# Interleaved map rows, a split rotary swap and earlier value splits in the projection of a hybrid attention kernel

## The reference, cut to what matters

```python
def partial_rope(t, positions):
    half = ROPE_DIM // 2          # ROPE_DIM = 16, half = 8
    ...
    x1, x2, rest = tf[..., :half], tf[..., half:ROPE_DIM], tf[..., ROPE_DIM:]
    return jnp.concatenate([x1 * cos - x2 * sin, x2 * cos + x1 * sin, rest], axis=-1)

proj = h @ w_in[layer]
dq = proj[..., :o1].reshape(b, s, 2 * DIFF_HEADS, HEAD_DIM)     # HEAD_DIM = 64
dk = proj[..., o1:o2].reshape(b, s, 2 * DIFF_HEADS, HEAD_DIM)
dv = proj[..., o2:o3].reshape(b, s, DIFF_HEADS, DIFF_V_DIM).astype(f32)
dq = partial_rope(dq, positions)
dk = partial_rope(dk, positions)
```

## Time and profile before

| | us |
|---|---|
| median of 3 runs (lowest, highest) | 3023.31 (3022.39, 3024.48) |
| the profiled execution, its time | 3015.76 |
| the profiled execution, its span (first to last instruction) | 3013.7 |
| TensorE matmuls (PE) busy | 2917.5, 97% of the span |
| VectorE (DVE) busy | 1972.6, 65% |
| ScalarE (ACT) busy | 1586.0, 53% |
| GpSimd (POOL) busy | 913.2, 30% |
| granted TensorE clock, mean | 0.994 of full speed |

### The profile page before, as it was taken

How to read it: one execution, slowest core, us unless ns; L and a number is a source line. 1 busy time by engine, 2 the same in 40 slices (tenths; PEclk the granted TensorE clock), 3 DMA queues, 4 the chain that set the end, 5 groups by cost and what they waited for, 6 DMA issues and landing times.

```text
span 3013.7 us, 51920 instructions
## 1 busy us (share of the span) xinstructions
PE 2917.5 (97%) x19000; PEld 2610.4 (87%) x19000; DVE 1972.6 (65%) x2944; ACT 1586.0 (53%) x2672; POOL 913.2 (30%) x1022
## 2 busy tenths in 40 slices
PE   7999989899999999999999999999999999999998
PEld 6888778787777999999889998998889998999886
DVE  6215520177676777778568786886658878888656
ACT  5122211267767878888545554554445555655444
POOL 1922221055665877777301221111000000001100
PEclk9999999999999999999999999999999999999999
DMA  5488895556643541501339998999746775699954
GB/s 206 123 212 206 206 234 131 128 114 149 149 108 66 122 88 25 113 32 61 109 126 286 315 308 255 281 274 311 213 131 217 233 237 182 217 327 295 286 191 157
DMA packets 303481, 559.47 MB, mean 186 GB/s; under 512 B 32288, under 2 KB 70304, under 8 KB 302112
## 3 DMA queue, kind: packets, MB, share of 16 engines
q1 hardware_dynamic: 263936, 464.17, 48.6%
q0 software_dynamic: 39072, 92.30, 16.0%
q10 hardware_dynamic: 288, 0.59, 0.1%
HBM read 449.98 MB, written 197.13 MB: 215 GB/s over the span
## 4 chain that ended last, share of the span: by engine, by line
PE 61%; DVE 9%; POOL 5%; ACT 3%; issue 2%; DMA 1%; DVEq 0%; SPq 0%; ACTq 0%; POOLq 0%
PE f_ps L2428 28%; PE f_ps L2320 18%; PE h_o L996 6%; PE h_t L982 3%; PE h_z L718 2%; PE h_z L721 2%; POOL h_work L1280 2%; DVE h_negmax L1116 2%; POOL h_more L1280 2%; DVE h_more L1232 2%; DVE h_more L1148 1%; ACT h_more L1015 1%; ACT h_work L1015 1%; POOL h_srstd L1325 1%; PE h_o L939 0%
## 5 line engine op out<-in xcount | busy, mean ns | idle before, releaser
L1807 ACT ACTIVATE f_whi<-f_wraw 128x512 fp32r<-128x512 f32 x834 | 520.9, 627 | 420.0 <-PE f_ps L2428 288.9
L1814 DVE TENSOR_TENSOR f_wlo<-f_wraw,f_whi 128x512 fp32r<-128x512 f32 x834 | 574.8, 690 | 240.8 <-ACT f_whi L1807 237.7
L2428 PE MATMUL f_ps<-f_hi_s,f_whi 128*128 128x256 f32 x1408 | 397.3, 282 | 4.7 <-DVE f_up L2161 4.7
L2428 PE MATMUL f_ps<-f_lo_s,f_whi 128*128 128x256 f32 x1408 | 397.2, 282 | 0.0
L2428 PE MATMUL f_ps<-f_hi_s,f_wlo 128*128 128x256 f32 x1408 | 396.5, 282 | 0.0
L1320 POOL TENSOR_TENSOR h_work<-h_work,h_more 128x1024 f32<-128x1024 f32 (+3 forms) x192 | 302.6, 1589 | 110.0 <-DVE h_more L1232 97.2
L2428 PE MATMUL f_ps<-f_hi_a,f_whi 128*128 128x256 f32 x1056 | 298.3, 282 | 1.1 <-DVE f_second L2161 0.8
L2428 PE MATMUL f_ps<-f_lo_a,f_whi 128*128 128x256 f32 x1056 | 297.9, 282 | 0.0
L2428 PE MATMUL f_ps<-f_hi_a,f_wlo 128*128 128x256 f32 x1056 | 297.7, 282 | 0.0
L2428 PEld LDWEIGHTS f_ps<-f_hi_s,f_whi 128*128 128x128 f32 x1408 | 267.6, 190 | 5.6 <-DVE f_wlo L1814 3.1
L2428 PEld LDWEIGHTS f_ps<-f_hi_s,f_wlo 128*128 128x128 f32 x1408 | 267.6, 190 | 0.0
(11 more groups left out here) (199 smaller groups left out, 6874.2 us busy)
## 6 DMA issues: line engine op xcount, KB each, us to landing
f_wraw<-in_w_stream SPq DMA_DIRECT2D x394, 256.0 KB, 4.0
f_wraw<-sums_scratch SPq DMA_DIRECT2D x352, 256.0 KB, 4.4
sums_scratch<-in_w_stream POOLq DMA_DIRECT2D x132, 256.0 KB, 5.4
act_scratch<-f_act SPq DMA_DIRECT2D x88, 256.0 KB, 3.8
combined_acts<-f_act SPq DMA_DIRECT2D x88, 256.0 KB, 4.7
f_wraw<-down_sums SPq DMA_DIRECT2D x88, 256.0 KB, 2.7
f_piece<-combined_acts SPq DMA_DIRECT2D x88, 256.0 KB, 2.9
down_sums<-in_w_stream POOLq DMA_DIRECT2D x66, 256.0 KB, 6.5
```

The lines of the kernel that those rows point to most:

```text
L1807: act.activation(w_hi[ring][:], w_raw[ring][:], ACT.Copy).then_inc(S["hi_split"], 1)
L1814: dve.tensor_tensor(w_lo[ring][:], w_raw[ring][:], w_hi[ring][:].bitcast(F32), ALU.subtract).then_inc(S["lo_split"], 1)
L2428: mm = pe.matmul(outs[i], w[ring][:, col], a[name][:, c, :], start=(c == 0 and m == 0), stop=(c == 3 and m == 2))
```

## The change

- The columns of the query and key weights are reordered ahead of the run, for all 16 tiles: row 2y + m of a tile is now row y of map m. The first halves of both maps (8 rows each) are then rows 0 to 15, the second halves rows 16 to 31. `inv_freq` follows.
- The store writes the rows back in their old order in memory: its memory side is given as (64 rows, 2 maps, 512 tokens). Nothing that reads the scratch changes. All 64 units are stored this way.
- The swap is two transfers of 16 rows: second halves to first by SP, first halves to second by ScalarE's queue, right behind the copy, with a wait for that copy. The counts on `swapped` fall from 64 to 32 per unit.
- VectorE makes raw times cosine first, after the copy and ahead of the wait for the transfers; sine is multiplied into `swapped_qk` in place.
- `V_SPLITS` gives one value split to each of units 57 to 61 and two to unit 62; splits 3 to 5 wait for the sum of a unit and not for its low part; value loads 4 to 7 are issued behind units 57 to 60, one each.
- ScalarE waits once, ahead of unit 32, for the cleared `swapped_qk`.

```diff
--- before.py
+++ after.py
@@ -68,7 +68,8 @@
 UNITS = TILES * BLOCKS
 HALVES = 2 * TPB
 TURNED = HEAD_DIM // 8
-V_SPLITS = {UNITS - 6: (0,), UNITS - 5: (1,), UNITS - 4: (2, 3), UNITS - 3: (4,), UNITS - 2: (5, 6)}
+FIRST_HALVES, SECOND_HALVES = slice(0, 2 * TURNED), slice(2 * TURNED, 4 * TURNED)
+V_SPLITS = {UNITS - 7: (0,), UNITS - 6: (1,), UNITS - 5: (2,), UNITS - 4: (3,), UNITS - 3: (4,), UNITS - 2: (5, 6)}
 
 
 SUM_OPS = 8
@@ -192,18 +193,14 @@
                 n, b = unit_of(o)
                 sp.wait_ge(unit_done, BLOCKS + o + 1)
                 for part_no, src in ((0, out_hi), (1, out_lo)):
-                    sp.dma_start(qk_scratch[part_no, n * P:(n + 1) * P, b * BLK:(b + 1) * BLK],
-                                 src[:, b, :].bitcast(F32)).then_inc(stored[b], 16)
+                    rows = qk_scratch[part_no, n * P:(n + 1) * P, b * BLK:(b + 1) * BLK]
+                    sp.dma_start(rows.rearrange("(m y) t -> y m t", m=2), src[:, b, :].bitcast(F32)).then_inc(stored[b], 16)
 
             def swap(o):
 
 
-                slot = o % 2
                 sp.wait_ge(raw_copied, o - FIRST_ROT + 1)
-                for first in range(0, P, HEAD_DIM):
-                    for to, source in ((first, first + TURNED), (first + TURNED, first)):
-                        sp.dma_start(swapped_qk[to:to + TURNED, slot, :], raw_qk[source:source + TURNED, slot, :])\
-                          .then_inc(swapped[slot], 16)
+                sp.dma_start(swapped_qk[FIRST_HALVES, o % 2, :], raw_qk[SECOND_HALVES, o % 2, :]).then_inc(swapped[o % 2], 16)
 
             def load_v(n):
                 if 4 <= n < KC:
@@ -258,9 +255,8 @@
                     if FIRST_ROT <= n * BLOCKS + b < UNITS - 1:
                         swap(n * BLOCKS + b + 1)
                     store(n * BLOCKS + b)
-                    if n >= TILES - 2 and b in (0, 3) and n * BLOCKS + b != (TILES - 2) * BLOCKS and n * BLOCKS + b < UNITS - 1:
-                        for k in range(2):
-                            load_v(2 * (n - TILES + 4) + k)
+                    if UNITS - 7 <= n * BLOCKS + b < UNITS - 3:
+                        load_v(n * BLOCKS + b - UNITS + 11)
             for n in range(KC, 12):
                 load_v(n)
             for b in range(BLOCKS):
@@ -367,6 +363,8 @@
                 act.wait_ge(projected, o + 2)
                 act.activation(raw_qk[:, b % 2, :], bank[b][:], ACT.Copy, scale=SCALE if kind_of(n) == "dq" else 1.0)\
                    .then_inc(raw_copied, 1)
+                act.wait_ge(raw_copied, o - FIRST_ROT + 1)
+                act.dma_start(swapped_qk[SECOND_HALVES, b % 2, :], raw_qk[FIRST_HALVES, b % 2, :]).then_inc(swapped[b % 2], 16)
 
             def rotated_hi(o):
                 n, b = unit_of(o)
@@ -383,7 +381,7 @@
                 elif n == 2:
                     act.wait_ge(projected, (TILES - 1) * BLOCKS + 1)
                 elif n < 6:
-                    act.wait_ge(unit_done, UNITS + n - 2)
+                    act.wait_ge(summed, UNITS - FIRST_ROT + n - 6)
                 elif n == 6:
                     act.wait_ge(unit_done, UNITS + 3)
                 elif n == KC - 1:
@@ -438,6 +436,8 @@
                     if o < FIRST_ROT:
                         plain_hi(o)
                         continue
+                    if o == FIRST_ROT:
+                        act.wait_ge(rest_cleared, 1)
                     raw_copy(o)
                     if o > FIRST_ROT:
                         rotated_hi(o - 1)
@@ -488,10 +488,11 @@
                 rot = o - FIRST_ROT
                 sin, cos = sinT[:, b * BLK:(b + 1) * BLK], cosT[:, b * BLK:(b + 1) * BLK]
                 slot = (slice(None), b % 2, slice(None))
-                dve.wait_ge(swapped[b % 2], 64 * (rot // 2 + 1))
-                link(dve, dve_chain, rot * 2 + 1, dve.tensor_tensor(turned_qk[slot], swapped_qk[slot], sin, ALU.mult))
-                link(dve, dve_chain, rot * 2 + 2, dve.tensor_tensor(raw_qk[slot], raw_qk[slot], cos, ALU.mult))
-                dve.tensor_tensor(turned_qk[slot], turned_qk[slot], raw_qk[slot], ALU.add).then_inc(summed, 1)
+                dve.wait_ge(raw_copied, rot + 1)
+                dve.tensor_tensor(turned_qk[slot], raw_qk[slot], cos, ALU.mult).then_inc(dve_chain, 1)
+                dve.wait_ge(swapped[b % 2], 32 * (rot // 2 + 1))
+                link(dve, dve_chain, rot * 2 + 2, dve.tensor_tensor(swapped_qk[slot], swapped_qk[slot], sin, ALU.mult))
+                dve.tensor_tensor(turned_qk[slot], turned_qk[slot], swapped_qk[slot], ALU.add).then_inc(summed, 1)
                 dve.wait_ge(summed, rot + 1)
                 dve.wait_ge(stored[b], n * 32 + 32)
                 dve.wait_ge(hi_out, o + 1)
@@ -2586,8 +2587,8 @@
                 sb_norm_g, w_out, norm_ffn_g, w_gate, w_up, w_down, final_norm_g):
 
     chunked = w_in[0].reshape(KC, P, -1)
-    w_qk = np.stack([chunked[:, :, COL[kind] + f * P:COL[kind] + (f + 1) * P].transpose(1, 0, 2)
-                     for kind in QK_ORDER for f in range(QK_TILES)])
+    w_qk = np.stack([chunked[:, :, COL[kind] + f * P:COL[kind] + (f + 1) * P].reshape(KC, P, 2, HEAD_DIM)
+                     .transpose(1, 0, 3, 2).reshape(P, KC, P) for kind in QK_ORDER for f in range(QK_TILES)])
     w_v = np.stack([chunked[:, :, COL[kind]:COL[kind] + GROUP] for kind in ("dv", "sv")])
 
     def natural(w):
@@ -2602,10 +2603,9 @@
 
     half = TURNED
     inv_freq = np.zeros((P, 1), np.float32)
-    for first in range(0, P, HEAD_DIM):
-        for i in range(half):
-            inv_freq[first + half + i] = np.float32(500000.0) ** np.float32(-i / half)
-            inv_freq[first + i] = -inv_freq[first + half + i]
+    for row in range(4 * half):
+        turn = np.float32(500000.0) ** np.float32(-(row // 2 % half) / half)
+        inv_freq[row] = turn if row >= 2 * half else -turn
     row, col = np.arange(P)[:, None], np.arange(P)[None, :]
     return dict(
         x=x[0], positions=positions, g_attn=norm_attn_g, w_qk=w_qk, w_v=w_v, w_stream=w_stream,
```

## The result

| | kernel before | changed kernel |
|---|---|---|
| median of the timed comparison | 3022.85 us (4 runs, 3015.83 to 3024.48) | 3000.18 us (4 runs, 2999.52 to 3001.45) |
| ratio, 95% interval | | 0.993 (0.9913 to 0.9947) |
| profiled execution, span | 3015.76, 3013.7 us | 3000.31, 2998.2 us |

The forecast was 3008 us in a range of 3003 to 3016: the sign was right and the size too small. By the profiled executions the change brings 15.5 us, by the medians 22.7. That gap is what the experiments had to explain.

The account below looks back on a forecast made before the run. TensorE, busy 97%, bounds the kernel, so only its projection gaps could be won: -7.5 - 12.9 + 4 + 1.2 = -15.2 us, from the 3023.31 median to 3008, range 3003 to 3016.

Parts of the forecast that it names:

- loss A: Rotated query and key units 32 to 63: 7.5 us over TensorE's own pace, forecast to go entirely.
- loss B: First value group: 12.9 us lost to two waits on value splits and a slow clock, forecast to shrink to 4.
- A + B = 20.4 us is the most: Projection stage: loss A plus loss B, 20.4 us, claimed as the most this change can give.
- T + 5.5: Forecast end of unit 62's low part, in us, T being unit 63's end; value tile 5 waits for it.
- The clock behind the wait: Value products: slow TensorE clock after the remaining 4 us wait, half of 13 slow matmuls by 0.18 us, 1.2 us.
- Cosine, 0.73 per pair: Rotated units on VectorE: cosine product done during the swap transfer takes 0.73 us off each pair of chains.
- the rival of 3012: Swap gains nothing from fewer transfers and a second queue, only the cosine counts: gain 11 us, 3012; chance 0.20.
- Two transfers on two queues: Swap of rotated units: issued 2.0 us sooner, of which 1.2 us per pair counts, within bounds 0 and 2.0.
- the 10.1 us: Forecast cost of a pair of rotated chains, 11.97 - 0.73 - 1.2 + 0.1, under TensorE's 11.09.
- Bound landing: Rival: swap landing is set by transfers ahead, so sooner issue buys nothing; gain 8 to 13 us; chance 0.20.
- The slower rival: Permuted store served like the key loads, 9.1 us to landing against 5.9: +26 us, 3050; chance 0.07.
- Passed on whole: From the projection's end to the kernel's end: whole gain arrives, 2 us allowed; rival that it does not, 0.08.

Follow-up runs that it names:

- before_again: Kernel before, unchanged, run again for its scatter: median 3020.2 us, ratio 0.9997; its profiled execution 3017.5 us.
- before_p1: Kernel before, unchanged, one further profiled execution: 3020.5 us.
- after_again: Changed kernel, unchanged, run again with more executions: median 2999.0 us, ratio 0.9927 to the kernel before; its profiled execution 2993.3 us.
- cos_only: Kernel before with only the cosine product moved ahead of the wait for the transfers: median 3006.6 us, ratio 0.9944.
- old_cos: Changed kernel with the cosine product back behind the wait and the sine: median 3011.8 us, ratio 0.9958 to the kernel before.
- rows_only: Kernel before with only the row order, two swap transfers from two queues and three-dimensional stores: median 3008.5 us, ratio 0.9957.
- four_two_queues: Changed kernel with old row order, old stores and four 8-row transfers, two of them issued by ScalarE: median 3001.9 us, ratio 0.9944 to the kernel before.
- before_p2: Kernel before, unchanged, one more profiled execution: 3026.9 us.

## Why the prediction was wrong

Two steps of the prediction failed: the size of loss A, which it read in one execution, and the end of unit 62's chain, which sized what is left of loss B. By the means of the profiles (four of before, three of the changed kernel) the stage ends 20.1 us sooner where the sum gave 15.2. Loss A gave 9.7 us of it (7.5 forecast) and the value part 10.6 (7.7 forecast); the start of the stretch lay 0.3 us later. The further 2.6 us up to the 22.7 of the medians lie behind the stage or in the choice of executions; they are not told from chance.

- **Which base the gain was taken from: wrong.** "I take the difference from the median" joined two things that do not belong together: the losses of one execution of 3015.8 us and a median of 3023.3. Of that distance a part is loss in the very stage that is changed: its end is 583.2 in this execution and 584.4 to 589.3 in the three others, and loss A is 7.5, 10.6, 7.5 and 12.9 us. It does not follow the total strictly (before_again ended its stage at 587.8 and took 3017.5, before_p1 584.4 and 3020.5), since what follows scatters too.
- **The hit on its own base is luck in part.** Taken from its own execution, the sum of 15.2 gives 3000.6 for the profiled run, which was 3000.31. But the stage gave 13.3 of it and not 15.2, and 2.2 came behind the stage, where the forecast had nothing.
- **"A + B = 20.4 us is the most": wrong for the same reason.** It was the most of that execution. The four profiles of before lose 20.4 to 26.5 us, taking 562.8 (583.2 - 20.4) as the floor; the range's lower end, 3003, stood on this.
- **Loss A goes: right.** The stretch of units 32 to 63 takes TensorE's own pace in all three profiles of the changed kernel, with no L574 wait.
- **Loss B shrinks to 4: right in one profile, too large in two.** For tile 5 the prediction took unit 62 to lag like unit 63, by 11 us, its low part ending at "T + 5.5", and 1 us later with value load 7. Measured, it ends at T + 6.4, T + 2.9 and T + 3.4, and the value wait is 3.2, 0 and 0.5 us. The two chains that run side by side do not lag alike: in after_again unit 63 lags by 10.0 us, within the "10 to 11" forecast, but unit 62 by 8.4 (2.9 and the unit's 5.5), and tile 5 is ready in time.
- **The clock behind the wait, 1.2 us: too small where there was a wait.** 2.9 us behind 3.2 of wait; none in the other two.
- **Cosine, 0.73 per pair: right in the chain.** From the sine's start to the low part's end it is 2.91 us where it was 3.63, and cos_only's pair is 11.17 against 11.24. Its worth was under-told by the rival of 3012: alone it brings 3006.6.
- **Two transfers on two queues, 1.2 us per pair: the size cannot be read from the pair, the reason was wrong.** At TensorE's pace the pair says no more what a chain costs, so the 10.1 us is not shown. In copy to sine the two queues give 1.6 us or more, but old_cos lies only 0.7 us under before. I put it on issue time. On one queue half the transfers change nothing (11.92 against 11.97), although SP issues 1.2 us in place of 2.65.
- **Bound landing, 0.20: right in one half.** ScalarE's transfers land no sooner, as it said; that the second queue would then gain nothing is refuted by rows_only.
- **Store with three dimensions: small, as taken.** Issues are 0.53 and 0.60 us against 0.32 and 0.43, +0.4 per pair of stores (0.1 forecast, 0.6 its bound); landing 6.3 against 5.9. The slower rival, landing like the key loads, did not come. four_two_queues, with the old stores, lies within 2 us of the changed kernel.
- **ScalarE's issue at nothing: right.** 0.51 to 0.63 us each, and no TensorE wait on ScalarE in the stage.
- **Passed on whole: right within the scatter.** The first profiles gain 13.3 us at the end of the stage and 15.5 at the end of the span.

## What to carry to other kernels

A loss read in a profile belongs to the execution it was read in: subtract it from that execution's time, profile the kernel several times, and before a ceiling is called one, look at how far the timed runs lie from the profiled one. Where a chain of small steps runs just over the pace of the engine that matters, compare the chain's period with that engine's period first. Here either of two steps alone, one product moved ahead of a wait (16.6 us) or half of the swap moved to a second queue (12.4 us, with the new rows), brought the chains near that pace, and both together 21 to 23: such gains do not add up.

## What the runs showed that was not expected

A second issuing queue whose transfers land no sooner (4.9 against 4.7 us) still took the kernel from 3017.7 to 3008.5 us. And a wait of 3.0 us on TensorE went with a granted clock of 0.58 of full speed in the 5 us around its end, where waits of up to 2.0 us had left it at 1.00. The length of the wait alone does not decide: waits of 2.25 us in before_again and 2.33 in before_p2 went with 0.83 and 0.82, one of 2.89 us in old_cos left the clock at 1.00. In the changed kernel's first profile wait and slow clock together cost 6.1 us.
